# Products of zeros on TensorE between the first eleven units of a three-mixer transformer kernel

## The reference

```python
x = first_block(...)       # layer 0: short gated convolution and gated delta rule (GDN), 8 heads of 128
                           # layer 1: HGRN2, 16 heads of 128; after each a layer norm and a gate
return second_block(x, ...)  # sliding-window attention, then relu(h @ w_up)**2 @ w_down

def conv_gdn_mixer(x, ...):
    proj = x @ w_in                                   # 1024 x 8208
    qkv = silu(causal_depthwise_conv(qkv, conv_b_w))  # 4 taps
    q, k = l2_normalize(q), l2_normalize(k)
    o = gated_delta_rule(q, k, v, g, beta)            # chunks of tokens, triangular solve
    ...
    return concatenate([y_a, o], -1) @ w_out
```

## Time and profile before

| | |
|---|---|
| median of 3 runs | 944.72 us (943.66 to 947.94) |
| span of the profiled execution | 941.9 us |
| smallest time shown less that span | 1.8 us |
| TensorE busy | 909.3 us, 97% |
| GpSimd busy | 676.8 us, 72% |
| ScalarE busy | 505.8 us, 54% |
| VectorE busy | 475.5 us, 50% |
| mean granted TensorE clock | 0.998 |

### The profile page before, as it was taken

One profiled execution on the slowest core, in us unless ns is written; L12 is line 12 of the kernel. 1 busy time (PEld: TensorE's weight loads), 2 busy tenths in 40 slices (PEclk: granted clock), 3 DMA queues, 4 the chain that ended last, 5 costly groups with the idle time before them and its releaser, 6 DMA issues.

```text
span 941.9 us, 19627 instructions
## 1 busy us (share of the span) xinstructions
PE 909.3 (97%) x7790; PEld 840.5 (89%) x7790; DVE 475.5 (50%) x975; ACT 505.8 (54%) x711; POOL 676.8 (72%) x486
## 2 busy tenths in 40 slices
PE   5799899999999999999999999999999999999997
PEld 5799899988999788999999999888897799998886
DVE  3437855359554163567877767726646352221004
ACT  3576542483324555657766677556567365554341
POOL 3688555565655777977677776768798569889983
PEclk9999999999999999999999999999999999999999
DMA  4678355555543656664455544565663247656641
GB/s 158 178 235 171 109 135 115 115 139 122 133 130 113 200 168 179 185 189 123 134 156 165 150 140 134 155 208 151 188 210 110 93 129 223 196 185 200 203 134 45
DMA packets 133300, 146.14 MB, mean 155 GB/s; under 512 B 11022, under 2 KB 100056, under 8 KB 133208
## 3 DMA queue, kind: packets, MB, share of 16 engines
q1 hardware_dynamic: 131224, 140.64, 51.7%
q10 hardware_dynamic: 1984, 4.24, 1.4%
HBM read 143.81 MB, written 1.05 MB: 154 GB/s over the span
## 4 chain that ended last, share of the span: by engine, by line
PE 82%; DVE 5%; POOL 3%; issue 3%; ACT 3%; DMA 3%; SPq 1%; DVEq 0%; ACTq 0%; POOLq 0%
PE dense L569 23%; PE dense L570 22%; PE dense L571 22%; DMA raw<-in_w_in_even_dram 3%; PE bank L946 2%; POOL wlo L544 2%; POOL wlo L543 2%; PE bank L839 1%; PE bank L835 1%; PE bank L854 1%; ACT whi L1205 1%; DVE cv L1795 1%; PE dense L638 1%; PE bank L978 1%; PE bank L932 1%
## 5 line engine op out<-in xcount | busy, mean ns | idle before, releaser
L544 POOL TENSOR_TENSOR wlo<-raw,whi 128x512 fp32r<-128x512 f32 (+1 forms) x263 | 415.1, 1587 | 25.5 <-ACT whi L1205 25.4
L543 POOL TENSOR_TENSOR wlo<-raw,whi 128x512 fp32r<-128x512 f32 x199 | 258.7, 1300 | 208.5 <-ACT whi L1205 208.2
L1205 ACT ACTIVATE whi<-raw 128x1024 fp32r<-128x1024 f32 x264 | 276.1, 1058 | 240.0 <-PE dense L571 190.3
L569 PE MATMUL dense<-x_hi,whi 128*128 128x256 f32 x1232 | 352.6, 286 | 13.3 <-POOL wlo L538 5.8
L570 PE MATMUL dense<-x_lo,whi 128*128 128x256 f32 x1232 | 343.8, 279 | 0.0
L571 PE MATMUL dense<-x_hi,wlo 128*128 128x256 f32 x1232 | 343.6, 279 | 0.0
L569 PEld LDWEIGHTS dense<-x_hi,whi 128*128 128x128 f32 x1232 | 232.9, 189 | 19.1 <-issue 10.0
L570 PEld LDWEIGHTS dense<-x_lo,whi 128*128 128x128 f32 x1232 | 233.8, 190 | 0.7 <-issue 0.2
L571 PEld LDWEIGHTS dense<-x_hi,wlo 128*128 128x128 f32 x1232 | 232.7, 189 | 0.0
L569 PE MATMUL dense<-whi,ya_hi 128*128 128x512 f32 x192 | 77.3, 403 | 1.0 <-issue 0.8
L571 PE MATMUL dense<-whi,ya_lo 128*128 128x512 f32 x192 | 75.0, 391 | 0.0
(11 more groups left out here) (342 smaller groups left out, 1433.4 us busy)
## 6 DMA issues: line engine op xcount, KB each, us to landing
raw<-in_w_in_odd_dram SPq DMA_DIRECT2D x64, 512.0 KB, 3.9
raw<-in_w_in_even_dram SPq DMA_DIRECT2D x32, 512.0 KB, 8.7
raw<-in_w_in_even_dram SPq DMA_DIRECT2D x64, 256.0 KB, 4.5
raw<-in_mlp_w_up_dram SPq DMA_DIRECT2D x32, 512.0 KB, 3.7
raw<-in_mlp_w_down_dram SPq DMA_DIRECT2D x32, 512.0 KB, 4.5
raw<-in_w_out_even_dram SPq DMA_DIRECT2D x16, 512.0 KB, 3.9
raw<-in_w_pl_gate_dram SPq DMA_DIRECT2D x16, 512.0 KB, 4.5
raw<-in_w_out_odd_dram SPq DMA_DIRECT2D x16, 512.0 KB, 4.0
```

The source lines that it names most:

```text
L543: pool.tensor_tensor(wlo[:, slot, 0:half], unit_slot(u)[:, 0:half], whi[:, slot, 0:half].bitcast(F32), ALU.subtract)
L544: pool.tensor_tensor(wlo[:, slot, first:2 * half], unit_slot(u)[:, first:2 * half], whi[:, slot, first:2 * half].bitcast(F32), ALU.subtrac ...
L569: pe.matmul(out_, lh, rh, start=start, stop=False, skip_group_check=True)
L1205: act.activation(whi[:, u % NSPL, :], unit_slot(u), ACT.Copy).then_inc(hi_done, 1)
```

## The change

A tile `idle_w` of 128 x 1024 is set to zero by VectorE at the very start. TensorE waits for that, multiplies parts of the tile by other parts, and lets the products fall into PSUM banks SB[2] and SB[3], where nobody reads them. Seven products of 512 columns stand ahead of the first transposes, 45 of 256 columns behind them, and then a batch behind each of the units 1 to 10. The batches differ in where their operands lie, in whether the columns are read in chunks, in the width of the stationary operand (16 or 128) and in the bank. The batch comes directly behind the unit, before the small pieces of work that stand there.

```diff
+        idle_w = sb("idle_w", [P, 1024], F32R)
+        idle_zero = sem("idle_zero")
...
+            def idle_products(first, columns, moving, count, bank=2, other=2):
+                n = moving.shape[1] * (moving.shape[2] * moving.shape[3] if len(moving.shape) == 4 else 1)
+                for i in range(count):
+                    o = SB[other if i % 2 else bank][0:columns, 0:n]
+                    if len(moving.shape) == 4:
+                        o = o.rearrange("p (c h w) -> p c h w", h=moving.shape[2], w=moving.shape[3])
+                    pe.matmul(o, idle_w[:, first:first + columns], moving, start=(i < 2), stop=(i >= count - 2), skip_group_check=True)
+            def idle_chunks(w):
+                return idle_w[:, 256:512].rearrange("p (h c w) -> p c h w", h=2, w=w)
+            IDLE = {1: (0, 16, idle_w[:, 256:512], 10), 2: (0, 16, idle_w[:, 272:528], 10), 3: (0, 16, idle_chunks(16), 10),
+                    4: (0, 16, idle_chunks(8), 10), 5: (0, 16, idle_chunks(32), 10), 6: (0, 16, idle_w[:, 256:512], 10, 2, 3),
+                    7: (0, 128, idle_w[:, 256:768], 6), 8: (0, 16, idle_w[:, 256:768], 6), 9: (0, 128, idle_chunks(16), 10),
+                    10: (0, 128, idle_w[:, 256:512], 10, 2, 3)}
+            pe.wait_ge(idle_zero, 1)
+            idle_products(0, 128, idle_w[:, 256:768], 7)
             pe.wait_ge(consts_loaded, 16)
             transposes("x_t", 0, xtok, x_loaded[0], [32, 32], range(1))
+            for off in (0, 16, 32, 48, 8):
+                idle_products(0, 128, idle_w[:, 256 + off:512 + off], 9)
...
                     out_unit("out_even", n - FIRST_OUT)
+                if n in IDLE:
+                    idle_products(*IDLE[n])
                 if n == 2:
...
+            vec.memset(idle_w[:, :].bitcast(F32), 0.0).then_inc(idle_zero, 1)
+            settle(idle_zero)
             take("x_t", 0, xf0, x_hi, x_lo, 0, parts=range(2))
```

## The result

| | before | after |
|---|---|---|
| median of 12 runs, us | 945.07 (943.54 to 950.06) | 950.04 (947.67 to 954.49) |
| ratio | | 1.005, 95% interval 1.003 to 1.0069 |
| span of the profiled execution, us | 941.9 | 949.3 |
| mean granted clock | 0.998 | 0.994 |
| TensorE busy, us | 909.3 | 930.2 |

The kernel became slower by 5.0 us, where 4.3 were forecast. The ratio sits on the half per cent, so whether it is "slower by over 0.5%" can't be told. The profiled executions lie 7.4 us apart, more than the medians, because the one before (943.66 us) lies 1.4 us under its median and the one after (951.12 us) 1.1 us over it. The mean granted clock also counts half clock behind the last matmul, 1.2 us of it before (from 940.7) and 3.8 us after (from 945.5), where TensorE has nothing left to do; the matmuls end at 935.9 and 943.3.

The account below looks back on a forecast made before the run. TensorE, busy for 97% of the span, was taken as the bound once weights are ready, from unit 8. Uncovered batches 5.0, unit 7's delay 0.2, less 0.9 absorbed: +4.3 us, 944.72 to 949.0; 8-in-10 range 945.6 to 951.4.

Parts of the forecast that it names:

- The bound and the place of the cost: TensorE sets the pace from unit 8 on, so batches behind units 7 to 10 cost their full 5.0 us.
- the signs named beforehand: Changed profile: unit 7 within 0.5 us of 42.82, unit 8 about 1.4 us late, first GDN product 4.3 late (83.4).
- The durations: TensorE products start to start: 0.1133 us for 256 columns, 0.230 for 512; 16 stationary columns no cheaper than 128.
- The start: Products ahead of unit 0 end near 11.7 us, before 12.40; unit 0 saves 1.2 us, lost at the next wait; gain nothing.
- The rival that zeros do not raise the clock: Ahead of unit 0: 45 products last until 16.5 us, about 2 us more reach unit 7; 951 us, chance 0.10.
- Units 1 to 6: Idle times before the next units absorb most of these batches, 1.13 us each; unit 7 starts 0.1 to 0.8 us late.
- so I take 0.2: Delay taken for the start of unit 7, from a range of 0.1 to 0.8 us: 0.2 us.
- What was absorbed: TensorE's 0.92 us wait for ScalarE before the first GDN product swallows 0.9 us of the delay.
- The sum: Whole kernel: 5.0 + 0.2 - 0.9 = +4.3 us, profiled span from 941.9 to 946.2.
- The clock rival: Timed runs fall to half clock between units 1 and 7; products prevent it: 944.5 us, or 942.9; chance 0.12.
- Absorption: The half-clock stretch at 111.25 may not recur, or VectorE gets ahead from 79 to 92: +2.6, 947.3 us; chance 0.15.
- one more fall: One additional fall of the clock, place not named: +5.9, 950.6 us; chance 0.13.

Follow-up runs that it names:

- GDN 26: 26 products of 256 columns ahead of the GDN step at unit 23, no other added products, against the kernel before; 941.74 us, ratio 0.9984.

## Why the prediction was right, point by point

**The bound and the place of the cost** were right. After unit 7 TensorE has no room, before it it has. The kernel with batches 7 to 10 alone has the GDN at +3.9 and a ratio of +4.1 us, against 5.0 - 0.9 = 4.1 reckoned; the batches themselves take 2 x 1.39 + 2 x 1.20 = 5.2 us. Of the signs named beforehand, those at unit 7 and behind it missed: unit 7 is 1.7 us late for at most 0.5, unit 8 (48.75) 3.1 for 1.4, and the first GDN product stands at 84.85 for 83.4.

**The durations** were right to 1 and 6 per cent: 0.232 us for 0.230, and 0.120 for 0.1133. The estimates from the Trainium skill ("TensorE: Matmul & The Clock Gate", section "Wait — 56ns, not 53.3ns?"), 0.216 and 0.109 us, lie further off, and the sum of 4.1 us that they give too. A stationary operand of 16 columns saved nothing, as read from the gate columns, and reading in chunks cost nothing.

**The start** was right: the clock rises in time, and what is won in unit 0 meets the next wait. The rival that zeros do not raise the clock fell with the 0.118 us of the 45 products: it had them at half clock all the way, 0.213.

**Units 1 to 6** were mis-sized. The step "so I take 0.2" for unit 7 measured 1.7 us in the profile after. It has two parts. From unit 5 to unit 7 the list took 44.53 - 35.64 = 8.89 us where before 42.82 - 34.28 = 8.54 us passed: 0.35, inside the bounds given. The other 1.36 us is unit 5 itself, which started at 35.64 for 34.28 because its weights landed late. ScalarE's rounding of units 4 and 5, in its timeline after:

```profile
27.16 1.06 ACT L1230 ACTIVATE whi<-raw 128x1024 fp32r<-128x1024 f32 x1 [3.87 <-DMA raw<-in_w_in_even_dram]
31.92 1.06 ACT L1230 ACTIVATE whi<-raw 128x1024 fp32r<-128x1024 f32 x1 [2.83 <-DMA raw<-in_w_in_even_dram]
```

The same rows before:

```profile
26.11 1.06 ACT L1205 ACTIVATE whi<-raw 128x1024 fp32r<-128x1024 f32 x1 [3.40 <-DMA raw<-in_w_in_even_dram]
30.58 1.06 ACT L1205 ACTIVATE whi<-raw 128x1024 fp32r<-128x1024 f32 x1 [2.54 <-DMA raw<-in_w_in_even_dram]
```

ScalarE waits for the DMA in both. Over the fourteen profiles the rounding of unit 4 is later than 27 us in three, and these are three of the four kernels with both the start products and the batches 1 to 4; in the other eleven it is 26.24 at the latest. Most of it lies in the transfer and not in the issue: SyncE issued this load at 10.9 to 11.4 us in the three, at 11.2 before and at 10.3 to 10.8 in the other ten, and it took 15.8 to 16.7 us to land in the three, 14.9 before and 14.9 to 15.9 in the other ten. The prediction held the supply to be independent of TensorE. Neither part alone shows the delay. But the pattern was noticed after the fact, rests on one profile per kernel, and the fourth kernel with both (start, 1 to 4) has neither the delay nor a cost in its ratio. Why the loads took longer was not found. It stays open, chance included.

**What was absorbed** before the GDN was 1.33 us for 0.9: from unit 11 to the first GDN product 22.61 us passed before (56.53 to 79.14) and 21.28 after (63.57 to 84.85). The 0.92 us wait is in it; the other 0.4 are matmuls that followed each other more closely.

**The sum at the profile.** 1.71 for unit 7, 5.33 from unit 7 to unit 11, less 1.33: +5.71 at the GDN. The grant was at half for 6.8 us instead of 3.4, which makes 1.7 more, 7.4 together, which is the difference of the spans. Without the late weights (1.36) and the longer fall (1.7) 4.3 us are left, the forecast's sum. That it fits so well is partly luck: the three terms measured 0.35, 5.33 and 1.33 for 0.2, 5.0 and 0.9, and the errors cancel. The medians are 5.0 us apart. For the clock, the timed runs show that executions differ: the mean grant runs from 0.992 to 0.999 over the twelve runs after, and the profiled one had 0.994. How many had late weights is not known. The ratios of the parts do not add up either: 2.3 us for the start and 1 to 6, 4.1 for 7 to 10, together 6.4, where the whole has a ratio of 1.005, 4.7 us. The wait before the GDN, of which each part alone can use some, explains up to 0.9 of that; the rest is within the intervals.

**The clock rival** was right that the clock falls before unit 7, and too small in the time. The clock does fall before unit 7 in some executions: in three of the eight profiles without batches behind units 1 to 4 (7 to 10, the same doubled, GDN 26), and in one of the six with them, during unit 6, where no batch stood behind unit 5. That products behind the units prevent such falls is not shown: three of eight against none of six while the batches stood there is too few. The batches 1 to 4 alone came out at 0.9984, 1.5 us under before (0.9968 to 0.9999), the most that any run shows of this rival. It did not bring back the 4.1 us behind unit 7. The GDN's wait of 2.1 us cost the clock in nine of ten profiles without products there and in none of the four with them; the later waits, 1.2 or 1.0 us and then 0.8, cost it in six of fourteen; the gaps of 1.2 to 1.5 us before the units mostly did not. The rule of the Trainium skill ("TensorE: Matmul & The Clock Gate", section "HAM oscillation — how this bites in real kernels") that waits between short bursts bring the clock down again and again fits the GDN's wait better than it fits the units.

**Absorption and one more fall** both occurred in single executions: the kernel with start and 1 to 6 has no fall at the GDN's first waits (it has one at 233.5 us), the kernel after has a double one. As sizes for the medians neither was needed.

## What to carry to other kernels

Keeping TensorE busy with products that nobody reads is free where a wait covers them, and behind the point where TensorE sets the pace every product costs its whole time; count the batch against the idle time before the next instruction, and stop at the first unit that finds its weights ready. Where TensorE and another engine take turns, count against the other engine's chain and not against the next matmul: 13 products too many in the GDN made one step 1.5 us late and the kernel no longer. Put the products where the granted clock is seen to fall on the chain that sets the end (here a wait of 2 us in the GDN, worth 1.5 us), and look for the same step later on: it cost 1.5 us again in six of fourteen profiles, and nobody filled it. Where the supply sets the pace, half clock costs little. When a DMA's landing ends the wait, the cover is not the same twice: in the ten profiles without both start products and batches 1 to 4 the rounding of unit 5 began anywhere from 29.03 to 30.80 us, so a batch that just fills the gap in one profile will stick out in the next.

## What the runs showed of the hardware

- Products of zeros keep the granted clock up as others do: 0.118 us per 256 columns from 6.9 to 12.2 us, against 0.213 in unit 0 of the kernel before. Seven of them and eight transposes stood ahead of the rise.
- A matmul of 512 columns takes 0.232 us start to start with a stationary operand of 128 or of 16 columns.
- While there was work on TensorE, the grant fell for 3.4 us or 6.8 us, nothing between. The same program differs in this from execution to execution: the mean grant of the kernel before runs from 0.991 to 0.999 over its timed runs.
- Waits of 1.2 and 0.8 us with a matmul step between them were followed by half clock in six of nine profiles (228 to 245 us), waits of 0.97 and 0.77 us at the same place in none of five.
- The load of unit 4 took 15.8 to 16.7 us to land in three of four kernels with many products both before unit 0 and behind units 1 to 4, and 14.9 to 15.9 in the ten others; its rounding began about 1.3 us later. The cause is open.
